# The triangular inverse of a gated delta rule: three of its six matrix levels become a substitution on VectorE

## The reference

```python
gc = jnp.cumsum(blocks(g), axis=-1)
low = jnp.einsum('nbhik,nbhjk->nbhij', kb, kc) * decay_strict
eye = jnp.eye(chunk, dtype=jnp.float32)
t_inv = lax.linalg.triangular_solve(low + eye, jnp.broadcast_to(eye, low.shape),
                                    left_side=True, lower=True, unit_diagonal=True)
u = jnp.einsum('nbhij,nbhjv->nbhiv', t_inv, vb)
w = jnp.einsum('nbhij,nbhjk->nbhik', t_inv, kb * jnp.exp(gc)[..., None])
# then, chunk after chunk:
v_new = u_ - w_ @ s
o = (q_ * exp(g_)) @ s + a_ @ v_new
s = s * exp(g_last) + k_dec.T @ v_new
```

## Time and profile before

| | |
|---|---|
| time, median of 3 runs (lowest, highest) | 1866.65 us (1863.89, 1868.72) |
| the profiled execution's own time | 1866.97 us |
| its span | 1865.2 us |
| granted clock of TensorE, mean | 0.996 |
| busy: PE, PEld, DVE, ACT, POOL | 97%, 92%, 42%, 32%, 11% |
| DMA | 225.36 MB, all but 1 MB on one hardware queue |

### The profile page before, as it was taken

One profiled execution on the slowest core, in us unless ns is written; L12 is line 12 of the kernel. 1 busy time (PEld: TensorE's weight loads), 2 busy tenths in 40 slices (PEclk: granted clock), 3 DMA queues, 4 the chain that ended last, 5 costly groups with the idle time before them and its releaser, 6 DMA issues.

```text
span 1865.2 us, 33692 instructions
## 1 busy us (share of the span) xinstructions
PE 1806.5 (97%) x14152; PEld 1721.6 (92%) x14152; DVE 777.7 (42%) x1096; ACT 598.5 (32%) x920; POOL 206.2 (11%) x211
## 2 busy tenths in 40 slices
PE   6999998999999999999999999999999999999997
PEld 5999998999999999999999999999999997579997
DVE  5665445555454454545434344333311124332222
ACT  5554334242414324241422222222222223232222
POOL 0000000222222222222220000111100000001110
PEclk9999999999999999999999999999999999999999
DMA  7996733131213213121323333444443349533332
GB/s 216 271 256 195 196 102 93 47 105 47 81 51 98 74 53 101 49 81 46 96 72 83 94 81 103 130 136 138 145 136 91 112 165 412 170 101 102 107 95 102
DMA packets 321402, 225.36 MB, mean 121 GB/s; under 512 B 9785, under 2 KB 304450, under 8 KB 315858
## 3 DMA queue, kind: packets, MB, share of 16 engines
q1 hardware_dynamic: 321330, 224.33, 40.5%
HBM read 199.37 MB, written 25.30 MB: 120 GB/s over the span
## 4 chain that ended last, share of the span: by engine, by line
PE 86%; issue 4%; DVE 3%; DMA 3%; ACT 2%; POOL 1%; SPq 0%; ACTq 0%; DVEq 0%; POOLq 0%
PE pj L244 65%; PE dk L1112 2%; PE dk L1093 2%; DMA out_dram<-mst 2%; PE dk L1109 2%; PE dk L1985 2%; PE pj L2004 1%; ACT w_high L223 1%; PE dk L1916 1%; PE dk L317 1%; PE dk L1535 1%; PE pj L1927 1%; PE pj L2013 1%; DVE yq L833 1%; PE dk L1053 1%
## 5 line engine op out<-in xcount | busy, mean ns | idle before, releaser
L244 PE MATMUL pj<-a_hi,w_high 128*128 128x272 f32 x2560 | 556.4, 299 | 6.0 <-issue 4.2
L244 PE MATMUL pj<-a_hi,w_low 128*128 128x272 f32 x2560 | 530.4, 289 | 0.0
L244 PE MATMUL pj<-a_lo,w_high 128*128 128x272 f32 x2560 | 528.8, 288 | 0.0
L232 DVE TENSOR_TENSOR w_low<-w_raw,w_high 128x2048 fp32r<-128x2048 f32 x128 | 293.3, 2291 | 418.2 <-ACT w_high L223 418.1
L244 PEld LDWEIGHTS pj<-a_hi,w_high 128*128 128x128 f32 x2560 | 401.9, 189 | 17.8 <-issue 14.7
L244 PEld LDWEIGHTS pj<-a_lo,w_high 128*128 128x128 f32 x2560 | 403.1, 189 | 0.0
L244 PEld LDWEIGHTS pj<-a_hi,w_low 128*128 128x128 f32 x2560 | 401.0, 189 | 0.0
L223 ACT ACTIVATE w_high<-w_raw 128x2048 fp32r<-128x2048 f32 x128 | 244.4, 1909 | 1.6 <-DMA w_raw<-in_w_ck_dram 1.3
L244 PE MATMUL pj<-hm_hi,w_high 128*128 128x256 f32 x512 | 151.6, 296 | 0.5 <-DVE w_low L232 0.5
L244 PE MATMUL pj<-hm_hi,w_low 128*128 128x256 f32 x512 | 144.8, 283 | 0.0
L244 PE MATMUL pj<-hm_lo,w_high 128*128 128x256 f32 x512 | 144.8, 283 | 0.0
(11 more groups left out here) (376 smaller groups left out, 1961.7 us busy)
## 6 DMA issues: line engine op xcount, KB each, us to landing
w_raw<-in_w_in_dram SPq DMA_DIRECT2D x48, 1024.0 KB, 5.9
w_raw<-in_w_ck_dram SPq DMA_DIRECT2D x16, 1024.0 KB, 6.3
w_raw<-in_w_cv_dram SPq DMA_DIRECT2D x16, 1024.0 KB, 6.2
w_raw<-in_w_out_dram SPq DMA_DIRECT2D x16, 1024.0 KB, 6.1
w_raw<-in_w_cq_dram SPq DMA_DIRECT2D x16, 1024.0 KB, 6.0
w_raw<-in_w_co_dram SPq DMA_DIRECT2D x16, 1024.0 KB, 6.0
xr<-xT_scratch SPq DMA_DIRECT2D x16, 272.0 KB, 6.3
x2T_scratch<-x SPq DMA_DIRECT2D x16, 272.0 KB, 5.2
```

Source lines behind the costliest of these rows:

```text
L232: dve.tensor_tensor(low[q][:], raw[q][:], high[q % 2][:].bitcast(F32), ALU.subtract).then_inc(lo_split, 1)
L244: mm = pe.matmul(pj[:, 2 * (q % 2) + b, 0:n], wt[:, k, :], x(k, o, n), start=(k == 0 and m == 0), stop=(k == KT - 1 and m == 2))
```

## The change

Levels 1 to 3 and the old seed go. In their place the 16 x 16 blocks on the diagonal are inverted by forward substitution.

- `dve_delta`, phase 1: DVE masks `lt` to its strictly triangular 16 x 16 diagonal blocks (negated) and sums over the 8 block columns, which leaves `comp`: for each of the 128 rows 4 chunks and the sample matrix x 16 numbers.
- `act_delta`, phase 1: ACT stores `comp` (40 KB) to a DRAM scratch and, when that has landed, loads it back as `rep`: each partition gets the whole 16 x (5 x 16) of its block, 5,120 bytes, 640 KB in all. These are the first DMAs on ACT's queue. The cast of the next weights stands ahead of them.
- DVE meanwhile makes `at`, `kd` and the weight split. Then it runs `substitute`: 15 steps of a multiplication and an addition on 5 x (15 - j) numbers, each waiting for the one before. `spread` puts the columns back as block diagonal U and us. Then come `vb` and the first convolution.
- TensorE turns U (only the prompt's), then does levels 4, 5 and 6.
- `PLACE` has 27 steps instead of 33. `turn_u` moves from tile 1, k = 5 to tile 2, k = 3, and the output norm from tile 3, k = 13 to k = 15; `pe_ext` stands at k = 6, 12 and 4 of tiles 1, 2 and 3 instead of 2. On ACT the taking of tile 1's result moves into phase 2, behind level 4's copy; on POOL `pool_last` moves with it. Four of the level masks in the constants go, two masks and a small table come.

```diff
+        rep_d = nc.dram_tensor("rep_scratch", [P // BLK, BLK * (CH + 1) * BLK], F32, kind="Internal").ap()
...
+        rep = put("rep", [BLK, CH + 1, BLK], F32, take.pos[0] - 2 * CH * P)
...
-        def act_delta(act, n, q, cast, rows):
+        def act_delta(act, n, q, cast, rows, late_take=lambda: None):
...
             if q == 1:
+                cast()
+                act.wait_ge(comp_ready, n + 1)
+                act.dma_start(rep_d.rearrange("a (j f) -> (a j) f", j=BLK), comp[:].rearrange("p c i -> p (c i)")).then_inc(rep_stored, 16)
+                act.wait_ge(rep_stored, 16 * n + 16)
+                act.dma_start(rep[:].rearrange("p j c i -> p (j c i)"),
+                              rep_d.unsqueeze(1).to_broadcast([P // BLK, BLK, BLK * (CH + 1) * BLK])).then_inc(rep_loaded, 16)
+                rows()
+            if q == 2:
+                cast()
                 act.wait_ge(t0_done, n + 1)
...
+                for l in range(L0, LEVELS):
+                    act.wait_ge(p1_done, NLEV * n + l - L0 + 1)
                     act.activation(p1, dk[:, 0, :].rearrange("p (c n) -> p c n", c=CH), ACT.Copy).then_inc(p1_ready, 1)
+                    if l == L0:
+                        late_take()
+                rows()
...
+        def substitute(eng, n):
+            for j in range(BLK - 1):
+                eng.wait_ge(sub_step, NSUB * n + 2 * j + 1)
+                eng.tensor_tensor(xt[:, :, j + 1:BLK], rep[:, j, :, j + 1:BLK],
+                                  xs[:, :, j:j + 1].to_broadcast([P, CH + 1, BLK - 1 - j]), ALU.mult).then_inc(sub_step, 1)
+                eng.wait_ge(sub_step, NSUB * n + 2 * j + 2)
+                eng.tensor_tensor(xs[:, :, j + 1:BLK], xs[:, :, j + 1:BLK], xt[:, :, j + 1:BLK], ALU.add).then_inc(sub_step, 1)
...
+                dve.wait_ge(lt_ready, n + 1)
+                dve.tensor_tensor(uu, lt[:], per_chunk(cst[:, C_SUB:C_SUB + P]), ALU.mult)
+                dve.tensor_tensor(us[S_, :], lts[S_, :], cst[S_, C_SSUB:C_SSUB + NS], ALU.mult).then_inc(masked, 1)
+                dve.wait_ge(masked, n + 1)
+                dve.tensor_reduce(comp[:, 0:CH, :], uu.rearrange("p c (a i) -> p c i a", i=BLK), AX_X, ALU.add)
+                dve.tensor_reduce(comp[S_, CH, :], us[S_, :].rearrange("p (a i) -> p i a", i=BLK), AX_X, ALU.add).then_inc(comp_ready, 1)
...
+                start_columns(dve)
+                split()
+                dve.wait_ge(rep_loaded, 16 * n + 16)
+                substitute(dve, n)
+                spread(dve, n)
                 dve.wait_ge(v_turned, n + 1)
                 dve.tensor_tensor(vb, dk[:, 3, :].rearrange("p (c n) -> p c n", c=CH),
                                   hc[:, 1, 0:4].unsqueeze(2).to_broadcast([P, CH, P]), ALU.mult).then_inc(vb_ready, 1)
+                conv()
...
+            if q == 1:
+                pool.wait_ge(lt_ready, n + 1)
+                at_least(pool, p1_done, NLEV * n + 0)
+                pool.tensor_tensor(ltm[:], lt[:], per_chunk(lev(L0)), ALU.mult).then_inc(ltm_ready, 1)
+                old()
+            if q == 2:
+                at_least(pool, p1_done, NLEV * n + 1)
+                pool.tensor_tensor(ltm[:], lt[:], per_chunk(lev(L0 + 1)), ALU.mult).then_inc(ltm_ready, 1)
+                last()
...
         PLACE = [
-            (0, 6), (1, 0), (1, 5), (1, 6),
-            (1, 8), (1, 10), (1, 12), (1, 14), (2, 0), (2, 3),
-            (2, 4), (2, 6), (2, 8), (2, 10), (2, 11), (2, 13),
-            (2, 15), (3, 0), (3, 1), (3, 1), (3, 2), (3, 3), (3, 4), (3, 4), (3, 5),
-            (3, 6), (3, 7), (3, 8), (3, 8), (3, 9), (3, 10), (3, 10), (3, 13),
+            (0, 6), (1, 0), (2, 3), (1, 10),
+            (2, 5), (2, 7), (2, 8), (2, 10), (2, 12), (2, 14),
+            (3, 0), (3, 1), (3, 2), (3, 2), (3, 4), (3, 5), (3, 6), (3, 6), (3, 7),
+            (3, 8), (3, 9), (3, 10), (3, 10), (3, 11), (3, 12), (3, 12), (3, 15),
         ]
+        EXT_AT = {1: 6, 2: 12, 3: 4}
```

More of the change, by code:

```diff
@@ L48 @@
 LEVELS = 7
+BLK, L0 = 16, 4
 CSEG = 3 + NT
@@ L83, in constants @@
     c[:, C_INCL:C_INCL + P] = i >= j
-    for n in range(LEVELS):
-        c[:, C_LEV + n * P:C_LEV + (n + 1) * P] = level(1 << n, j, i) * (-1.0 if n == 0 else 1.0)
+    for n in range(L0, LEVELS):
+        c[:, C_LEV + (n - L0) * P:C_LEV + (n - L0 + 1) * P] = level(1 << n, j, i)
+    c[:, C_SUB:C_SUB + P] = -1.0 * ((i // BLK == j // BLK) & (i > j))
+    c[:, C_BLK:C_BLK + P] = i // BLK == j // BLK
+    c[:, C_E16:C_E16 + BLK] = j % BLK == np.arange(BLK)[None, :]
     j, i = j[:NS], i[:, :NS]
     c[:NS, C_SINCL:C_SINCL + NS] = (i // NT == j // NT) & (i >= j)
-    c[:NS, C_SL1:C_SL1 + NS] = -1.0 * level(1, j, i)
-    c[:NS, C_SL2:C_SL2 + NS] = level(2, j, i)
+    c[:NS, C_SSUB:C_SSUB + NS] = -1.0 * ((i // NT == j // NT) & (i > j))
     c[:NS, C_BM:C_BM + NB] = j // NT == np.arange(NB)[None, :]
@@ L567, in build @@
         x1 = take("x1", [3, CH, P])
+        rep = put("rep", [BLK, CH + 1, BLK], F32, take.pos[0] - 2 * CH * P)
+        take("rep_end", [BLK * (CH + 1) * BLK - 2 * CH * P])
         vbk = take("vbk", [2 * TOK])
-        smp = take("smp", [12, NS])
+        smp = take("smp", [9, NS])
         SQ = put("sq", [2, TOK], F32, M_DELTA + 8 * TOK + 3 * CH * P)
@@ L656, in pool_rows @@
             pool.wait_ge(x_turned, 48)
+            pool.memset(comp[:], 0.0)
             pool.memset(ab_f[:], 0.0).then_inc(ab_zero, 1)
@@ L869, in act_delta @@
             if q == 1:
-                act.wait_ge(t0_done, n + 1)
[L871 to L875, removed]
-                    act.activation(p1, dk[:, 0, :].rearrange("p (c n) -> p c n", c=CH), ACT.Copy).then_inc(p1_ready, 1)
[L877 to L882, removed]
+                cast()
[7 more added lines that the diff above has]
+                cast()
+                act.wait_ge(t0_done, n + 1)
+                act.activation(tt_, dk[:, 0, :].rearrange("p (c n) -> p c n", c=CH), ACT.Copy).then_inc(t_ready, 1)
+                for l in range(L0, LEVELS):
+                    act.wait_ge(p1_done, NLEV * n + l - L0 + 1)
+                    act.activation(p1, dk[:, 0, :].rearrange("p (c n) -> p c n", c=CH), ACT.Copy).then_inc(p1_ready, 1)
+                    if l == L0:
+                        late_take()
+                rows()
             if q == 3:
@@ L1008, in sample_r, with pool_delta @@
             dve.tensor_tensor(rt, tmp, betab[:, SEQ:TOK], ALU.mult).then_inc(rt_ready, 1)
-        POOL_OLD = (3, 6)
-        def pool_delta(pool, n, q, old):
+        def pool_delta(pool, n, q, old, last=lambda: None):
+            if q != 2:
+                last()
             if q == 0:
@@ L1024, in pool_delta @@
                 pool.wait_ge(lt_ready, n + 1)
[L1025 to L1032, removed]
+                at_least(pool, p1_done, NLEV * n + 0)
+                pool.tensor_tensor(ltm[:], lt[:], per_chunk(lev(L0)), ALU.mult).then_inc(ltm_ready, 1)
+                old()
+            if q == 2:
+                at_least(pool, p1_done, NLEV * n + 1)
+                pool.tensor_tensor(ltm[:], lt[:], per_chunk(lev(L0 + 1)), ALU.mult).then_inc(ltm_ready, 1)
+                last()
+                at_least(pool, p1_done, NLEV * n + 2)
+                pool.tensor_tensor(ltm[:], lt[:], per_chunk(lev(L0 + 2)), ALU.mult).then_inc(ltm_ready, 1)
+                old()
             if q == 3:
@@ L1185, in o_norm @@
                 mm.then_inc(osum_done, 1)
-            return [norms, gram, turn_u, turn_v] + [f(l) for l in range(1, LEVELS) for f in (level_p, level_u)] + [
+            return [norms, gram, turn_u, turn_v] + [f(l) for l in range(L0, LEVELS) for f in (level_p, level_u)] + [
                 v_new(0), state_o(0), sample_ks, state_k(1), v_new(1), state_o(1), state_k(2), sample_turn, v_new(2),
@@ L1267, in body @@
                     else:
-                        act_delta(act, h - 1, q, cast, rows)
-                    act_take(act, h, q)
+                        act_delta(act, h - 1, q, cast, rows, lambda: act_take(act, h, 1))
+                    if is_first(h) or q != 1:
+                        act_take(act, h, q)
             loop_heads(act, body)
@@ L1300, in body, with last @@
                 for q in range(4):
-                    if q > 0:
-                        pool_last(pool, h, q - 1)
+                    def last():
+                        if q > 0:
+                            pool_last(pool, h, q - 1)
+                    if is_first(h):
+                        last()
                     if is_first(h) and q == 3:
@@ L1310, in body @@
                     else:
-                        pool_delta(pool, h - 1, q, old)
+                        pool_delta(pool, h - 1, q, old, last)
             loop_heads(pool, body)
@@ L1318, in body @@
                     if q > 0:
-                        steps[q].setdefault(2, []).append(pe_ext(h, q - 1))
+                        steps[q].setdefault(EXT_AT[q], []).append(pe_ext(h, q - 1))
```

107 lines of the change are left out of this document (51 added, 56 removed).

## The result

| | before | after |
|---|---|---|
| time, median of 4 runs (lowest, highest) | 1866.20 us (1863.89, 1868.72) | 1847.62 us (1846.78, 1849.26) |
| after / before, 95% interval | | 0.9902 (0.9886 to 0.9918) |
| span of the profiled execution | 1865.2 us | 1844.7 us |
| granted clock of TensorE, mean | 0.996 | 0.981 |

The change makes the kernel faster by 18.6 us (1.0%). I had forecast 51 us, and the smallest gain in my range was 21. The sign was right; the size was wrong by 32 us.

What follows compares the result with a forecast made beforehand. TensorE, busy 97% of the span, was taken to bound the kernel. Savings of 86.6 us less new waits of 29.6 and 6.0 gave 51.0, so 1866.65 - 51 = 1815.7, 1816 us; range 1788 to 1846.

Steps and rivals of the forecast that it cites:

- What goes, 86.6 us: TensorE time saved over 8 heads: 74.0 us of level products and seed turning, 9.7 and 2.9 of waits.
- the turning without its sample part: Turning of the seed on TensorE: 0.44 us instead of 0.91, saving 0.47 per head.
- both waits: TensorE's waits at the convolution tail (L805, 9.7 us in seven heads) and a state product (L1133, 2.9 us) go.
- load 5.0: Load of 640 KB from the DRAM scratch: 5.0 us, taken between bounds of 3.5 and 6.1.
- Folded blocks at G + 6.05: DVE's masking and folding of the Gram product ends 6.05 us after that product's start on TensorE, G.
- Store and chain: Store of 40 KB to DRAM, 1.8 us; 30 dependent substitution operations on DVE, 7.2 us.
- The wait: TensorE waits at the turning of the seed for the inverted blocks: 3.7 us per head, 29.6 us in all.
- Rival B: TensorE's clock falls to its lower level behind the wait: 1.6 us per head, 13 us, time 1829; chance 0.15.
- The norms: Next head's norms wait for ACT since the output norm moves later: 0.85 us, 7 times, 6.0 us.
- Nothing else waits: Behind the turning of the seed, no level product on TensorE waits by more than the estimates' error.
- C: Rival: shorter store, load, chain and reduction hide the wait at the seed's turning; time 1786; chance 0.15.
- A: Rival: the 8-row load uses half the DMA engines, 6.3 us; 1.3 more per head, 10 us, time 1826; chance 0.2.

Runs made afterwards that it cites:

- e3_nosub: The changed kernel without its 30 substitution operations, so the inverse of the diagonal blocks isn't computed; store and load stay: 1778.25 us, ratio to before 0.9524.
- f1_busy26: The changed kernel with 26 unused products of constants on TensorE in front of its wait at the turning of the seed: 1831.63 us, ratio to before 0.9813.
- e1_rows16: The changed kernel with the folded blocks stored twice, so the load's source has 16 rows instead of 8: 1832.32 us, ratio to before 0.981.
- e2_busy: The changed kernel with 52 unused products of constants on TensorE in front of its wait at the turning of the seed: 1874.85 us, ratio to before 1.0037.

## Why the prediction was wrong

- **What goes, 86.6 us: held, and 8 too small.** The order of views led to it: TensorE bound, each product worth its time. The levels, the turning without its sample part and both waits came out; e3_nosub gives 89.3 + 5.4 (norms) = 94.7. Of the 8 us more, about 3 are two heads in which the kernel before had a lower clock (below). Some 2.6 more are the two waits themselves, for each holds TensorE up longer than its idle time says. In the kernel before, the last pair in front of the tail starts at 683.91 and the next piece of work was due 0.25 later, at 684.16; it starts 1.55 after that, where the view counts 1.39:

```profile
683.91 0.41 PE L244 MATMUL pj<-a_hi,w_low 128*128 128x272 f32 x2
685.71 0.27 PE L805 MATMUL pj<-cst,ext 128*3 128x128 f32 x1 [1.39 <-POOL ecol L782]
```

  Two waits x 0.16 x 8 heads are 2.6. Of the rest of some 2.5, 1.3 is that the kernel before itself ran 1.3 us longer beside e3_nosub (1867.54) than beside the changed kernel.
- **The term "load 5.0": failed.** It measured 7.7. I had both ends, 3.5 and 6.1, from transfers with 128 rows on both sides, and took a value near the middle. The Trainium skill, "DMA: Bandwidth & Descriptors", section "Why a DMA increments its semaphore by 16 and not by 1", says that a transfer takes the largest number of engines up to 16 that divides the slowest dimensions of both sides, 8 for this shape. The traces agree: shares of 0.48 with 8 rows and 0.95 with 16. I had written the rule down, and made it a rival with 0.2, and even there priced it at 6.3, though its own working reached 8.0. Cost: 2.5 x 8 = 20 us. With 16 rows the load takes 5.2, so the base figure was good.
- **Folded blocks at G + 6.05: 0.64 late**, 5 us over the heads. The reduction of 512 numbers took 1.04, not the 0.69 of an elementwise operation. The two masks took 1.9 together, where I had 1.50 for the large one and no price for the small one: the large one started before GpSimd's own mask and took 0.69, and the 32 by 32 one behind it fell under GpSimd's and took 1.27. A like operation on 32 by 32 (L1035), with GpSimd idle, takes 0.17 in e3_nosub.
- **Store and chain: right**, 0.3 and 0.2 shorter than reckoned. The unit from before's small operations, 0.20 and 1.07 ns per number, carried over to 30 operations that the trace had never shown. There is some luck in it: the 0.20 was read at 24 numbers, and I added the price of all numbers to it. Without counting those 24 twice the rows give 6.5, and 7.04 is measured.
- **The wait:** 3.7 + 2.5 + 0.64 - 0.34 - 0.2 = 6.3 per head, and 6.27 is measured in the head shown. Over all heads the profile counts 49.3, against 29.6 in the forecast; that is 20 us of the shortfall.
- **The clock, left out of the sum: failed.** Rival B priced 1.6 per head for a wait of 3.7; f1_busy26 gives 16 us over 8 heads, 2.0 each. I had argued against it that TensorE is busy for all of the 80 us around each wait; the clock came down all the same, behind every wait of 5.9 to 6.7 us (the changed kernel) and every one of 4.5 to 5.2 (e1_rows16). No run has the 3.7 that I forecast, so what such a wait costs isn't shown. The trace of before held a near case. I had read two waits in the stage of heads; there is a third, of 4.2 us, ahead of which TensorE was fully busy; it is the same before and after the change and so worth nothing in the sum. Behind it, from 285.3 to 288.3, the granted clock is 0.51:

```profile
PE pj L244 <- issue: 4.2, 1, 4.2
...
285.30:288.30 3.00, 2.96 (x13) 2.99 (x14) 2.86 (x5) 0.00 (x0) 0.00 (x0) 0.51 0.33 81
```

  With that row the rival deserved more than its 0.15.
- **The norms: right** (5.4 for 6.0). "Nothing else waits": right.
- **Two small slips in the rivals.** C's three savings (0.2, 1.5 and 0.6) leave 1.4 of the 3.7, not 1.2, and its own 1786 lies outside the range, which begins at 1788. Neither touches the result.

Together: e3_nosub lies 88.0 us under before's 1866.2, where the forecast without its wait has 80.6, so the gain side (norms included) gave 7.4 more. 51 + 7.4 - 19.7 (wait) - 16 (clock) = 22.7; 18.6 is measured. Of the 4 between, 1.3 are again the 0.16 by which each of the eight waits costs more than its idle time; the rest I haven't assigned. Both rivals were true at once. I had added them up only for the range's end (1839), and even that held A's low price.

The steps that failed are two terms of the sum: the load, put at 5.0 us where 7.7 are measured (20 us over the heads), and the clock behind the wait, put at nothing where it costs 2.0 us per head (16 us).

The changed kernel loses 69 us (1847.6 to 1778.3) between its three levels and what they could have given: 49 to 50 in waiting, 16 in the clock, and the same rest. Blocks of 8 by 8 win because the way through DRAM then fits under work that is there anyway.

## What to carry to other kernels

When TensorE bounds, price a chain that is to be hidden from the products' start to its consumer and find its slack first; a wait that is left costs its length, and behind waits of 4.5 us and more this kernel paid once more, 2 us behind those of 6, at half the clock. For a DMA whose shape the trace doesn't show, count the rows of the outermost dimension on both sides before taking a rate from transfers with 128. And choose the block size by what fits under the cover: half the block here took the load from 7.7 us to 2.6 and the chain from 7.0 to 3.0, for one more level of 2.7 us.

## What the runs showed of the hardware beyond that

- Filling a wait with useless products can pay: 26 of them in 6 us gave 16 us (f1_busy26); 52 cost 27 us against the changed kernel (e2_busy).
- The clock fell in the kernel before without a long wait too. Two heads took 84.1 us instead of 82.5, Gram product to Gram product. The stretches of one of them, columns as above:

```profile
618.00:622.00 4.00, 4.00 (x36) 4.00 (x35) 1.07 (x3) 1.17 (x4) 0.24 (x1) 1.00 0.01 1
622.00:626.00 4.00, 3.65 (x32) 3.42 (x30) 2.85 (x3) 1.38 (x1) 1.25 (x1) 1.00 0.94 254
626.00:630.00 4.00, 3.98 (x20) 3.83 (x21) 1.16 (x6) 0.42 (x2) 1.47 (x1) 0.57 0.04 10
```

The granted clock is 0.57 from 626 to 630. Before it lie 16 products with 8 columns (a state product) and the wait of 0.37 at L1133. Which of the two brings the clock down wasn't tried, nor why only two of eight heads show it, for all have both. In e3_nosub the narrow products stand in every head, the wait is gone, and so are the dips; that points to the wait but doesn't prove it.
- Folding 512 numbers to 64 by a strided reduction takes 1.04 us on DVE against 0.69 for an elementwise operation on 512; so the size of its input alone doesn't give its price. Whether the stride or the 64 results make the difference isn't shown.
